# Three reorderings at the edges of a layer, and ScalarE copies for the first group of a down-projection

## The reference, cut to what matters

```python
def rms_norm(x, g):
    xf = x.astype(jnp.float32)
    y = xf * lax.rsqrt(jnp.mean(xf * xf, axis=-1, keepdims=True) + EPS)
    return (y * g.astype(jnp.float32)).astype(x.dtype)

def swiglu(x, g, w_gate, w_up, w_down):
    n = rms_norm(x, g)
    return (jax.nn.silu(n @ w_gate) * (n @ w_up)) @ w_down
...
    for l in range(DEPTH):
...
        xp = xp + mix_output(o_a, o_lat, w_uv[l], gn_a[l], gn_b[l], w_out[l])
        xp = xp + swiglu(xp, ffn_norm[l], w_gate[l], w_up[l], w_down[l])
...
    y_prompt = rms_norm(xp, final_norm)
```

## Time and profile before

| | |
|---|---|
| median of 3 runs | 1434.56 us (1434.22 to 1435.37) |
| profiled execution, its time | 1433.07 us |
| profiled execution, its span | 1431.8 us |
| mean granted clock of TensorE | 0.997 |
| busy share of the span: PE, PEld, DVE, ACT, POOL | 98%, 92%, 79%, 51%, 11% |

### The profile page before, as it was taken

One profiled execution on the slowest core, in us unless ns is written; L12 is line 12 of the kernel. 1 busy time (PEld: TensorE's weight loads), 2 busy tenths in 40 slices (PEclk: granted clock), 3 DMA queues, 4 the chain that ended last, 5 costly groups with the idle time before them and its releaser, 6 DMA issues.

```text
span 1431.8 us, 24544 instructions
## 1 busy us (share of the span) xinstructions
PE 1398.7 (98%) x9278; PEld 1314.9 (92%) x9278; DVE 1124.8 (79%) x2032; ACT 732.1 (51%) x1472; POOL 157.6 (11%) x109
## 2 busy tenths in 40 slices
PE   7999999999999999999899999999999999999998
PEld 6897878999999999999888878699999999999998
DVE  5658667878799889889954776677797898988996
ACT  5458555434455455454544585643434544544555
POOL 2416020210000000000222241102000000000002
PEclk9999999999999999999999999999999999999999
DMA  5340221233022321322223211213221223222222
GB/s 171 109 116 12 73 75 40 74 103 104 30 89 67 111 75 60 103 89 74 74 84 117 76 55 47 76 45 107 71 74 60 82 76 110 72 76 89 89 67 96
DMA packets 142372, 115.27 MB, mean 81 GB/s; under 512 B 17808, under 2 KB 136976, under 8 KB 142224
## 3 DMA queue, kind: packets, MB, share of 16 engines
q1 hardware_dynamic: 142256, 113.71, 26.0%
HBM read 108.90 MB, written 6.62 MB: 81 GB/s over the span
## 4 chain that ended last, share of the span: by engine, by line
PE 80%; DVE 12%; ACT 3%; issue 3%; DMA 1%; SPq 1%; DVEq 0%; ACTq 0%
PE ps L670 18%; PE ps L1353 13%; PE ps L1354 13%; PE ps L1355 13%; PE ps L796 3%; PE ps L798 3%; PE ps L797 3%; DVE ringl L2501 2%; DVE xT L2535 2%; PE ps L1230 1%; PE ps L1121 1%; ACT pw L1487 1%; PE ps L720 1%; PE ps L911 1%; PE ps L1147 1%
## 5 line engine op out<-in xcount | busy, mean ns | idle before, releaser
L1857 ACT ACTIVATE ringh<-sums 128x512 fp32r<-128x512 f32 (+1 forms) x240 | 140.7, 586 | 135.6 <-DVE sums L2492 54.3
L1354 PE MATMUL ps<-tl,ringh 128*128 128x320 f32 x576 | 177.8, 309 | 0.0
L1355 PE MATMUL ps<-tth,ringl 128*128 128x320 f32 x576 | 177.5, 308 | 0.0
L1353 PE MATMUL ps<-tth,ringh 128*128 128x320 f32 x576 | 177.0, 307 | 0.0
L1353 PE MATMUL ps<-dhi,ringh 128*128 128x320 f32 x504 | 159.5, 317 | 13.4 <-DVE xT L2535 13.0
L2501 DVE TENSOR_TENSOR ringl<-sums,ringh 128x512 fp32r<-128x512 f32 (+1 forms) x240 | 152.6, 636 | 7.9 <-ACT ringh L1857 6.4
L1355 PE MATMUL ps<-dhi,ringl 128*128 128x320 f32 x504 | 156.2, 310 | 0.0
L2032 DVE TENSOR_TENSOR wlo<-wraw,whi 128x1024 fp32r<-128x1024 f32 (+1 forms) x69 | 79.3, 1149 | 79.4 <-ACT whi L1442 79.3
L1354 PE MATMUL ps<-dlo_rest,ringh 128*128 128x320 f32 x432 | 133.9, 310 | 0.0
L1354 PE MATMUL ps<-tbl,ringh 128*128 128x320 f32 x432 | 133.5, 309 | 0.0
L1355 PE MATMUL ps<-tbh,ringl 128*128 128x320 f32 x432 | 133.4, 309 | 0.0
(11 more groups left out here) (426 smaller groups left out, 3750.6 us busy)
## 6 DMA issues: line engine op xcount, KB each, us to landing
raw_gate<-w_gate SPq DMA_DIRECT2D x18, 1024.0 KB, 5.4
raw_up<-w_up SPq DMA_DIRECT2D x18, 1024.0 KB, 5.4
raw_gate<-w_down SPq DMA_DIRECT2D x12, 768.0 KB, 4.2
raw_up<-w_down SPq DMA_DIRECT2D x12, 768.0 KB, 4.2
wraw<-w_out SPq DMA_DIRECT2D x32, 128.0 KB, 2.9
wraw<-w_out SPq DMA_DIRECT2D x16, 256.0 KB, 3.1
wraw<-w_gate SPq DMA_DIRECT2D x8, 512.0 KB, 3.9
wraw<-w_up SPq DMA_DIRECT2D x8, 512.0 KB, 3.9
```

The source lines that it names most:

```text
L1353: mm(o, wh[:, c, :], xh[:, c, :], start=fresh and c == 0, stop=False, skip_group_check=True)
L1354: mm(o, wh[:, c, :], xl[:, c, :], start=False, stop=False, skip_group_check=True)
L1355: ins = mm(o, wl[:, c, :], xh[:, c, :], start=False, stop=c == (DP if down else KH) - 1, skip_group_check=True)
L1857: run(ring_of(n, x)[0], left_of(n, x), ACT.Copy).then_inc(a_hi.sem, 1)
```

## The change

Four edits. (1) In the first group of each part ScalarE copies the banks after products 1, 5 and 6 to k1, k5 and k2s; PE's products 6, 3 and 7 wait for these copies (kept), and VectorE adds k1, k5 and k2s to the residual two groups later (in part three one group later), after its own add of the same x. Only product 4 of a first group still waits for an add. (2) ScalarE: the squares of the first layer's result leave groups 27 to 29 and stand after the last chunk's high part, at the start of the second layer, with the high part of weight unit 2 among them; the second layer's own squares stay. (3) VectorE: the low part of weight unit 1 leaves the end of RUN and stands behind the low parts of chunks 0 to 3 of the next input. (4) PE, at the end of the program: the column sums of squares for tiles 2 to 4 stand ahead of the transposes of tile 2.

```diff
-KEPT = counts((1, 5, 6), 1)
-D_NEW = counts(range(1, 8), 1, NG, NG + NDOWN)
+def copied(n, x):
+    return x in (1, 5, 6) and (n < NG or (n - NG) % KH == 0)
+def added_with(n):
+    b, g = divmod(n - NG, KH)
+    return n - g if n >= NG and g == (1 if b == 2 else 2) else None
...
 def row_done(d):
     n = NG + 2 * KH + d // 2
-    return D_NEW[n, 4] if d % 2 else max(D_NEW[n, 2], D_NEW[n, 3])
+    return max(D_NEW[n, x] for x in ((5, 7, 4) if d % 2 else (1, 2, 6, 3)))
...
-                if down and x in (6, 3, 7, 4):
+                if down and (x == 4 or (x in (6, 3, 7) and (n - NG) % KH)):
                     pe.wait_ge(d_new.sem, d_new.at(l, D_NEW[n, {6: 1, 3: 5, 7: 6, 4: 7}[x]]))
...
-        pe.wait_ge(d_new.sem, d_new.at(DEPTH, 0))
-        y_turn(2, range(6))
-        pe.wait_ge(n_hi.sem, n_hi.at(DEPTH, 1))
-        pe.wait_ge(y_gained.sem, 2)
-        y_turn(2, range(6, 8)).then_inc(tile_turned.sem, 1)
         pe.wait_ge(sq_new.sem, sq_new.at(DEPTH, 3))
         for t in range(2, NT):
             ins = square_sums(3, t, [ssq, sq[:, 0], sq[:, 1]])
         ins.then_inc(stat_sum.sem, 1)
+        pe.wait_ge(d_new.sem, d_new.at(DEPTH, 0))
+        pe.wait_ge(n_hi.sem, n_hi.at(DEPTH, 1))
+        pe.wait_ge(y_gained.sem, 2)
+        y_turn(2, range(8)).then_inc(tile_turned.sem, 1)
...
-            run(sq[:, last % 2, :], xT[:, last, :], ACT.Square).then_inc(sq_new.sem, 1)
+            for c in range(0 if l else last, NC_):
+                act.wait_ge(ssq_new.sem, ssq_new.at(l, adds_before(c) - 6))
+                run(sq[:, c % 2, :], xT[:, c, :], ACT.Square).then_inc(sq_new.sem, 1)
+                if l and c == KH - 1:
+                    weight_hi(l, 2)
...
             def emptied(n, x):
-                if n >= NG:
-                    return
...
+                if n >= NG:
+                    if copied(n, x):
+                        gate_last = GROUPS_OF[(n - NG) // KH + 1][1] - 1
+                        act.wait_ge(a_used.sem, done)
+                        act.wait_ge(c_new.sem, c_new.at(l, C_NEW[gate_last, {1: 2, 5: 7, 6: 3}[x]]))
+                        out, bank = {1: (k1, bx), 5: (k5, by), 6: (k2s, bx)}[x]
+                        run(out[:, :], ps[:, bank, 0:HALF], ACT.Copy).then_inc(kept.sem, 1)
+                    return
...
                         if l == DEPTH - 1:
                             gained(c)
-                        squared(c)
+                            squared(c)
...
+                if not copied(n, x):
+                    dve.wait_ge(a_used.sem, a_used.at(l, STEP[n, x] + 1))
...
+                    vec.tensor_tensor(target, ps[:, bank, 0:HALF], target, ALU.add).then_inc(d_new.sem, 1)
+                first = added_with(n)
+                if first and x in (1, 5, 6):
+                    dve.wait_ge(kept.sem, kept.at(l, KEPT[first, x]))
+                    dve.wait_ge(d_new.sem, d_new.at(l, D_NEW[first, {1: 2, 6: 3, 5: 7}[x]]))
+                    earlier = xT[:, d, half(j)]
+                    vec.tensor_tensor(earlier, {1: k1, 5: k5, 6: k2s}[x][:, :], earlier, ALU.add).then_inc(d_new.sem, 1)
...
-                    if i + AHEAD < len(RUN) + 2:
-                        weight_lo(l + 1, i + AHEAD - len(RUN))
-                    else:
-                        next_low(i + AHEAD - len(RUN) - 2)
+                    if i == len(RUN) - AHEAD:
+                        weight_lo(l + 1, 0)
+                    elif i >= len(RUN) - 2:
+                        next_low(i - len(RUN) + 2)
...
-                for c in range(2, NC_ - 1):
+                for c in range(2, KH):
+                    next_low(c)
+                weight_lo(l + 1, 1)
+                for c in range(KH, NC_ - 1):
                     next_low(c)
```

More of the change, by code:

```diff
@@ L126, with residual_adds @@
 STEP = {key: q for q, key in enumerate(RUN)}
-KEPT = counts((1, 5, 6), 1)
 C_NEW = counts((3, 2, 7), 1)
 SILU = counts((2, 7, 4), 2)
-D_NEW = counts(range(1, 8), 1, NG, NG + NDOWN)
+def copied(n, x):
[3 more added lines that the diff above has]
+    return n - g if n >= NG and g == (1 if b == 2 else 2) else None
+def residual_adds():
+    for n, x in RUN:
+        if n >= NG and not copied(n, x):
+            yield n, x
+        if added_with(n) and x in (1, 5, 6):
+            yield added_with(n), x
+KEPT = {key: k + 1 for k, key in enumerate(key for key in RUN if copied(*key))}
+D_NEW = {key: k + 1 for k, key in enumerate(residual_adds())}
 RIGHT_OF = {1: 0, 5: 1, 6: 2, 2: 3, 3: 4, 7: 5, 4: 6}
@@ L1541, in _ @@
                         heads_out_act(8)
-                if u + 2 < WIN_U and (l, u) != (0, 0):
+                if 2 < u + 2 < WIN_U:
                     weight_hi(l, u + 2)
@@ L1875, in emptied @@
                         act.wait_ge(c_new.sem, c_new.at(l, C_NEW[n - 1, 2]))
+                    if n in (GROUPS_OF[2][0], GROUPS_OF[3][0]):
+                        act.wait_ge(d_new.sem, d_new.at(l, D_NEW[NG + KH * (n // 6 - 1), 1]))
                     run(k1[:, :], ps[:, bx, 0:HALF], ACT.Copy).then_inc(kept.sem, 1)
@@ L1880, in emptied @@
                         act.wait_ge(c_new.sem, c_new.at(l, C_NEW[n - 1, 7]))
+                    if n in (GROUPS_OF[2][0], GROUPS_OF[3][0]):
+                        act.wait_ge(d_new.sem, d_new.at(l, D_NEW[NG + KH * (n // 6 - 1), 5]))
                     run(k5[:, :], ps[:, by, 0:HALF], ACT.Copy).then_inc(kept.sem, 1)
@@ L1885, in emptied @@
                         act.wait_ge(c_new.sem, c_new.at(l, C_NEW[n - 1, 3]))
+                    if n in (GROUPS_OF[2][0], GROUPS_OF[3][0]):
+                        act.wait_ge(d_new.sem, d_new.at(l, D_NEW[NG + KH * (n // 6 - 1), 6]))
                     run(k2s[:, :], ps[:, bx, 0:HALF], ACT.Copy).then_inc(kept.sem, 1)
@@ L1983, in _ @@
                     next_high(c)
-                squared(NC_ - 2)
         def y_left_half(t):
@@ L2529, in down_emptied @@
                 q = DP * b + DP - 1
-                dve.wait_ge(a_used.sem, a_used.at(l, STEP[n, x] + 1))
-                if x in (2, 3, 7):
-                    dve.wait_ge(d_new.sem, d_new.at(l, D_NEW[n, {2: 1, 3: 6, 7: 5}[x]]))
                 target = xT[:, 2 * g + d, half(j)]
-                bank = bz if x == 2 else by if x in (5, 3) else bx
-                vec.tensor_tensor(target, ps[:, bank, 0:HALF], target, ALU.add).then_inc(d_new.sem, 1)
+                if not copied(n, x):
+                    dve.wait_ge(a_used.sem, a_used.at(l, STEP[n, x] + 1))
+                    if g and x in (2, 3, 7):
+                        dve.wait_ge(d_new.sem, d_new.at(l, D_NEW[n, {2: 1, 3: 6, 7: 5}[x]]))
+                    bank = bz if x == 2 else by if x in (5, 3) else bx
+                    vec.tensor_tensor(target, ps[:, bank, 0:HALF], target, ALU.add).then_inc(d_new.sem, 1)
[5 more added lines that the diff above has]
+                    vec.tensor_tensor(earlier, {1: k1, 5: k5, 6: k2s}[x][:, :], earlier, ALU.add).then_inc(d_new.sem, 1)
                 if g == 0 and x == 1:
```

3 lines of the change are left out of this document (1 added, 2 removed).

## The result

The changed kernel takes 1424.4 us, the median of 4 runs (1421.71 to 1426.02); before, 1434.39 (1432.49 to 1435.37). The ratio is 0.9932, with a 95% interval of 0.9915 to 0.995: 0.7% faster, a small change that is clear of the noise of these runs. A second set of runs gave 1423.76 and a ratio of 0.9926 (0.9913 to 0.9939).

A forecast was written before the change was run, and what follows sets the result against it. PE, busy 98% of 1431.8 us, bounds the kernel, so only its waits or slow clock can be won. 5.1 (copies) + 4.8 (seam) + 0 + 0 = 9.9 less than 1434.56 gives a median of 1424.7 us, range 1421.0 to 1430.0.

The forecast's parts named there:

- First groups: First groups of down-projections: with fewer VectorE adds queued, PE's products come earlier, 1.11 us a group, bounds 0.13 and 2.06.
- The third part of the second layer: Its first group: a late add starts ScalarE's scaling and squaring 0.45 later; the 1.11 is lost and 0.45 more.
- Two of its signs: PE's waits for VectorE's add fall from 13.0 us to about 2; second-layer (27, 4) still waits about 1.
- The seam: Between the layers: 0.62 at (28, 4), 2.87 at (29, 4), 1.14 for the halved clock, 0.17 behind; sum 4.8 us.
- The adds that come back: Two groups later VectorE makes three adds, 1.2 us, about 1.3 with lost overlap; taken to cost nothing.
- The moved squares: Start of the second layer: squares and adds done 19.5 after unit 0, in time by 1.3; cost 0, bound 0.9.
- The tail: End of the program: column sums ahead of transposes bring ScalarE's factors sooner, but output waits for the transposes; 0.
- rival (a): The tail's clock does not fall, so the transposes save 1.7 us more; 1423.0 us, chance 0.16.
- (b): First groups stay bound by VectorE and each wins only 0.13; 1429.6 us, chance 0.16.
- (d): Slower: VectorE's sum comes late, ScalarE's copy of (18, 6) waits behind it, every first group loses; 1441 us, chance 0.03.
- (c): Moved squares' adds collide with VectorE early in the second layer; PE waits 1.8 us at unit 2; 1426.5, chance 0.11.
- The price of an add beside VectorE: Beside GpSimd adds a low part took 2.32 instead of 1.23, so an add slows VectorE by 1.09, half its length.

The follow-up runs named there:

- same-group kernel: The changed kernel, but VectorE adds k1, k5 and k2s in the first group itself while PE still waits for ScalarE's copies alone; 1434.52 us.
- earlier copies: The changed kernel, but in first groups ScalarE copies bank 1 after products 1 and 6 one left-hand part sooner; 1424.6 us.
- squares-back profile: The changed kernel with edit 2 undone, the first layer's squares in groups 27 to 29 again; 1428.5 us.
- copies alone: The changed kernel with edits 2, 3 and 4 undone, so only edit 1 against before; 1430.16 us, ratio 0.9979.
- spread kernel: The changed kernel, but in the second layer's groups 27 and 28 ScalarE makes scaled chunks and squares one after each of four products; 1424.18 us.
- reorderings alone: The changed kernel without copies in a down-projection, so only edits 2 to 4 against before; 1427.87 us, ratio 0.9962.
- tail back: The changed kernel with edit 4 undone, the old order of column sums and transposes at the end; 1424.23 us.

## Why the prediction was right, point by point

- **First groups, 1.11 each.** The steps from product to product were forecast as 0.13, 0.81 in all at (18, 7), 1.02 at (18, 4), 1.11 at (19, 6). Measured in group 18: 0.14, 0.78, 1.00, 1.09. Five of six groups lie between 1.09 and 1.11. Group 22 of the second layer won 0.78: there (22, 7) waits 0.4 for the copy in k2s, which the re-timing of one group could not show. The reason held too: the same-group kernel shows that the gain needs the adds out of VectorE's queue, the earlier copies that this queue still bounds.
- **The third part of the second layer.** (27, 4) was to lose the group's 1.11 and 0.45 more, 1.56. Its step was 1.56. What followed was missed: behind the 2.64 us wait the clock fell, which cost 1.54, and the wait of (28, 4) before, with its 0.1, was no longer there, which gave 1.26. Net 1.8 instead of 1.56. In the squares-back profile, where the clock did not fall, the net was 27.44 - 25.87 = 1.57, as forecast. That the same block of squares stands in the first layer, and that edit 2 alone keeps the copies from paying for it there, the prediction did not say.
- **Two of its signs contradict its sum.** PE's waits for the add were to fall to about 2 us, and (27, 4) was to wait about 1. By the sum the wait at (27, 4) is 1.08 + 0.45 + 1.11 = 2.64, which is what was measured, and the waits came to 3.7. The sum was right here and the list of signs wrong.
- **The seam, 4.8.** Measured 0.52 + 0.11 at (28, 4), 2.91, 1.15 for the clock, 0.17 behind: 4.9. The prediction took the fall of the clock as a part of the wait. The copies alone had the wait without the fall, so 1.3 of the 4.9 belong to a fall that need not come.
- **The adds that come back: nothing.** No wait of PE in groups 20 and 24 for VectorE; right. The moved squares: forecast done 19.5 after unit 0, measured 732.05 - 712.36 = 19.69, in time by 1.13. Two misses cancel in it: the adds began 4.59 after unit 0 instead of 5.3, and took 15.1 instead of 14.2.
- **The tail: nothing.** Right, but rival (a) rested on a wrong price: in the three profiles of the new order whose clock stayed at 1.00 the end came at 14.77 to 14.82, no sooner than the 14.75 of after.
- **Rivals.** (b) fell: (18, 7) came 0.78 earlier, not 0.13. (d) fell with it. (c) fell: unit 2's low part is done at 722.78, and unit 2 starts only at 726.35, when the two units before it are through. At the layer's start the cover was VectorE's spare time: up to there two of its instructions met an add and lost 1.7 together, and VectorE stood idle 0.90 before unit 2's low part.
- **The price of an add beside VectorE.** The prediction read half an add from the earlier trace rows, and that was a misreading of a merged row. The two GpSimd adds there took 1.58 and 2.34 us. The low part of 1.23 began 0.34 behind the first and ended 1.08 behind its end, as if it had stood still until then. The second add began beside the low part and ended 1.40 behind it. The four slowed instructions of the spread kernel show the same, with their ends 0.41 or 0.42 behind those of the adds. The Trainium skill, page "SBUF — State Buffer", section "Who interferes with whom", has it that whichever of the two starts first holds a shared port pair for its whole length and the other is blocked. These ends agree with that. So what an instruction loses is the rest of the add that it meets, here 0.98 to 1.27 of 1.54 to 1.70, neither half an add nor, as the prediction's estimate by that page had it, a whole one.
- **The sum.** The terms in the trace are 5 x 1.11 less 0.3 for group 22, 4.9, less 0.7 for the third part: 9.45 where 9.9 was forecast; the medians say 10.0. From the first gate product to the end the two profiles of after are 8.2 and 8.3 us shorter than that of before. The smaller differences, such as 0.6 at (21, 7) of the second layer behind a load that came late, are of the kind that differs from run to run. The terms and their causes were right. That the median came within 0.3 of the forecast is luck: the four runs lie between 1421.71 and 1426.02, and the fall of the clock at the seam could have been absent.

## What to carry to other kernels

When one engine's queue is full in a short stretch, count what is taken out of that queue there, not how fast another engine does it: the same copies were worth 1.1 us a group with the adds deferred, and lost 0.9 with the adds left in place and waiting for the copies. A deferred step delays whoever waits for its end, so look for every consumer of it, and above all for one that stands ahead of urgent work in an in-order queue. Where one cause of a wait is removed, time the next one before counting the gain: ScalarE's block hid GpSimd's contention, and only removing both paid. Where a wait slows the clock behind it, follow the steps to the next wait before adding the two prices: here the slower products cost 1.54 and spared 1.26.

## What the runs showed of the hardware

- A VectorE instruction with two inputs in SBUF of 0.55 us took 1.53 to 1.82 beside a GpSimd add of 128x640, four times in the kernel with the pieces spread, and each ended 0.41 or 0.42 after the add; a low part of 1.22 took 2.32.
- The length of PE's wait alone did not decide the clock. The clock fell behind a wait of 3.49 us (before, at the seam) and behind one of 2.64 (after, at (27, 4)), and the products behind the wait took 1.15 and 1.5 us longer. It stayed at 1.00 behind a wait of 3.48 (copies alone, at the seam) and behind one of 2.64 (squares back, at (27, 4)), as it did behind 1.42 and 1.01.
- The windows of the tail's transposes had the clock at 0.57, 0.77 and 1.00 in before, after and tail back, and the stretch from (29, 4) to the end was 15.01, 14.75 and 15.04. In the reorderings alone it was 0.61 from 6 us behind (29, 4) on, and the stretch was 15.91.
